# Last expert pair of a two-layer decoder trunk: the residual enters the sums as identity products, and the output copies are shared by two engines

## The reference, cut to what matters

```python
x = x + mla_mixer(...)
h = rmsnorm(x, ffn_norm_o[i])
x = x + moe_swiglu(h, ...)      # the output of the program

# moe_swiglu: top 2 of 8 experts for each token
for e in range(N_EXPERTS):
    y = y + combine[:, e:e + 1] * (silu(ht @ w_gate[e]) * (ht @ w_up[e])) @ w_down[e]
```

## Time and profile before

| | us |
|---|---|
| median of 3 runs (lowest, highest) | 1339.09 (1338.69, 1341.25) |
| profiled execution | 1338.47 |
| its span, first to last instruction | 1336.3 |
| TensorE busy (share of the span) | 1276.0 (95%) |
| VectorE busy | 749.7 (56%) |
| ScalarE busy | 633.7 (47%) |
| mean of HBM traffic | 316 GB/s |

### The profile page before, as it was taken

One profiled execution on the slowest core, in us unless ns is written; L12 is line 12 of the kernel. 1 busy time (PEld: TensorE's weight loads), 2 busy tenths in 40 slices (PEclk: granted clock), 3 DMA queues, 4 the chain that ended last, 5 costly groups with the idle time before them and its releaser, 6 DMA issues.

```text
span 1336.3 us, 15885 instructions
## 1 busy us (share of the span) xinstructions
PE 1276.0 (95%) x6208; PEld 899.4 (67%) x6209; DVE 749.7 (56%) x933; ACT 633.7 (47%) x730; POOL 39.0 (3%) x48
## 2 busy tenths in 40 slices
PE   7987999999987989999999999999999999999997
PEld 6765788888875778475847565766656675838572
DVE  5876465444487458464727464736646543837370
ACT  5575562434358537263626353625444533626350
POOL 1012000000002200000000000000000000000000
PEclk9998999999998979999999999999999999999999
DMA  9632455364353458799999999999999999999996
GB/s 341 222 127 65 155 189 189 116 228 149 103 165 136 189 213 318 305 390 411 421 421 421 421 417 417 421 421 420 421 418 417 420 421 420 421 418 418 420 421 251
DMA packets 88757, 422.92 MB, mean 316 GB/s; under 512 B 8561, under 2 KB 15463, under 8 KB 57959
## 3 DMA queue, kind: packets, MB, share of 16 engines
q1 hardware_dynamic: 87468, 419.10, 79.5%
q0 software_dynamic: 992, 2.69, 0.6%
q10 hardware_dynamic: 218, 0.08, 0.0%
HBM read 420.77 MB, written 1.07 MB: 316 GB/s over the span
## 4 chain that ended last, share of the span: by engine, by line
PE 84%; DVE 7%; DMA 4%; ACT 3%; issue 2%; SPq 0%; DVEq 0%; ACTq 0%
PE PS L2151 12%; PE PS L2127 11%; PE PS L2131 11%; PE PS L2128 11%; PE PS L2143 7%; PE PS L1696 7%; PE PS L1700 7%; PE PS L1697 7%; DMA raw<-in_w_down_o_dram 3%; DVE w_r L954 2%; PE PS L2158 1%; PE PS L2067 1%; PE PS L2076 1%; ACT w_r L487 1%; PE PS L1815 1%
## 5 line engine op out<-in xcount | busy, mean ns | idle before, releaser
L1377 DVE TENSOR_TENSOR w_r<-raw,w_r 128x2048 fp32r<-128x2048 f32 (+1 forms) x150 | 314.8, 2102 | 179.3 <-ACT w_r L784 178.8
L784 ACT ACTIVATE w_r<-raw 128x2048 fp32r<-128x2048 f32 (+1 forms) x150 | 264.9, 1766 | 205.9 <-PE PS L2131 118.6
L2127 PE MATMUL PS<-w_r,a_hi 128*128 128x512 f32 x512 | 201.8, 394 | 0.0
L2128 PE MATMUL PS<-w_r,a_lo 128*128 128x512 f32 x512 | 199.9, 390 | 0.0
L2151 PE MATMUL PS<-raw,xs 128*64 128x512 f32 (+1 forms) x856 | 169.9, 543 | 0.0
L954 DVE TENSOR_TENSOR w_r<-raw,w_r 128x2048 fp32r<-128x2048 f32 (+4 forms) x69 | 139.3, 2044 | 40.2 <-ACT w_r L487 40.0
L1696 PE MATMUL PS<-w_r,a_hi 128*128 128x512 f32 (+4 forms) x384 | 144.4, 380 | 6.0 <-DVE a_lo L983 5.1
L1697 PE MATMUL PS<-w_r,a_lo 128*128 128x512 f32 (+4 forms) x384 | 141.9, 373 | 0.0
L487 ACT ACTIVATE w_r<-raw 128x2048 fp32r<-128x2048 f32 (+4 forms) x69 | 115.2, 1719 | 15.4 <-PE PS L1700 12.6
L2151 PEld LDWEIGHTS PS<-raw,xs 128*64 128x64 f32 x856 | 58.8, 137 | 92.8 <-issue 84.2
L2127 PEld LDWEIGHTS PS<-w_r,a_hi 128*128 128x128 f32 x512 | 96.2, 188 | 28.0 <-issue 8.5
(11 more groups left out here) (318 smaller groups left out, 1445.9 us busy)
## 6 DMA issues: line engine op xcount, KB each, us to landing
raw<-in_w_down_o_dram SPq DMA_DIRECT2D x94, 1024.0 KB, 18.8
raw<-in_w_gate_o_dram SPq DMA_DIRECT2D x53, 1024.0 KB, 14.6
raw<-in_w_up_o_dram SPq DMA_DIRECT2D x51, 1024.0 KB, 15.1
raw<-in_w_gate_o_dram SPq DMA_DIRECT2D x53, 768.0 KB, 12.1
raw<-in_w_up_o_dram SPq DMA_DIRECT2D x53, 768.0 KB, 11.7
slots<-in_w_down_o_dram SPq DMA_DIRECT2D x18, 1024.0 KB, 18.3
raw<-in_w_in_e_dram SPq DMA_DIRECT2D x12, 1024.0 KB, 10.5
raw<-in_w_down_e_dram SPq DMA_DIRECT2D x11, 1024.0 KB, 4.8
```

Source lines behind the costliest of these rows:

```text
L784: nc.scalar.activation(w_r[:, high_slot(g), 0:w], place_of(n)[:, 0:w], ACT.Copy).then_inc(hi_done, 1)
L1377: nc.vector.tensor_tensor(place_r(n)[:, 0:w], place_of(n)[:, 0:w], w_r[:, high_slot(g), 0:w], ALU.subtract).then_inc(lo_done, 1)
L2127: nc.tensor.matmul(PS[:, bank, :], xh(x), hi[:, c0:c0 + NT], start=first, stop=False)
L2128: nc.tensor.matmul(PS[:, bank, :], xl(x), hi[:, c0:c0 + NT], start=False, stop=False)
```

## The change

In the last pair TensorE makes back_large four chunks earlier (behind k = 84), and behind it four more products, ident times the matching piece of X, into the same four banks. The sums that back_small closes therefore hold the new X already. VectorE's four additions go; VectorE copies banks 0 and 2 to X, ScalarE copies banks 1 and 3. A new semaphore out_act counts ScalarE's copies, and the stores, TensorE's last wait and the spare pass wait for both counts. The spare pass, which this input doesn't run, uses the semaphores raw_full in place of seven of its own.

```diff
+        F_SPARE = [16 * len(range(i, C_MOE, RAW)) for i in range(RAW)]
+        LAST_ADDS = 4 * (PAIRS - 1) + 2
@@ SyncE @@
-                    .then_inc(sem(f"spare_full{slot}"), 16)
+                    .then_inc(raw_full[slot], 16)
...
             for s in range(4):
                 t, half = s // 2, s % 2
-                sp.wait_ge(sem("moe_add"), 4 * (PAIRS - 1) + s + 1)
+                sp.wait_ge(sem("out_act" if half else "moe_add"), t + 1 if half else 4 * (PAIRS - 1) + t + 1)
@@ ScalarE, end of pair(p, follow) @@
                 small_result(p)
+                if not follow:
+                    for s in (1, 3):
+                        act.wait_ge(sem("moe_sc"), 4 * p + s + 1)
+                        nc.scalar.activation(X[:, s // 2, NT:D], PS[:, LAST_BACK[s], :], ACT.Copy).then_inc(sem("out_act"), 1)
@@ VectorE, end of pair(p, follow) @@
                 if not follow:
-                    for s in range(4):
-                        add_back(p, s, LAST_BACK[s])
+                    for s in (0, 2):
+                        dve.wait_ge(sem("moe_sc"), 4 * p + s + 1)
+                        nc.vector.tensor_copy(X[:, s // 2, 0:NT], PS[:, LAST_BACK[s], :]).then_inc(sem("moe_add"), 1)
@@ TensorE, pair(p, follow) @@
-                    if not follow and k == PAIR_CHUNKS - 4:
+                    if not follow and k == PAIR_CHUNKS - 8:
                         pe.wait_ge(sem("s_es"), 4 * p + 4)
                         back_large(p, LAST_BACK)
+                        pe.wait_ge(sem("moe_add"), 4 * p)
+                        for s in range(4):
+                            nc.tensor.matmul(PS[:, LAST_BACK[s], :], ident, X[:, s // 2, s % 2 * NT:(s % 2 + 1) * NT],
+                                             start=False, stop=False)
@@ TensorE, behind the last pair @@
-            pe.wait_ge(sem("moe_add"), 4 * PAIRS)
+            pe.wait_ge(sem("moe_add"), LAST_ADDS)
+            pe.wait_ge(sem("out_act"), 2)
```

More of the change, by code:

```diff
@@ L450, in _ @@
             with sp.If(most > 0):
-                sp.wait_ge(sem("moe_add"), 4 * PAIRS)
+                sp.wait_ge(sem("moe_add"), LAST_ADDS)
+                sp.wait_ge(sem("out_act"), 2)
                 with sp.Fori(0, NE) as e:
@@ L461, in _ @@
                         for slot in range(RAW):
-                            sp.sem_inc(sem(f"spare_full{slot}"), 16 * SPARE_CHUNKS // RAW)
+                            sp.sem_inc(raw_full[slot], 16 * SPARE_CHUNKS // RAW)
                 sp.wait_ge(sem("spare_add"), 4 * NE)
@@ L871, in pair @@
                 small_result(p)
+                if not follow:
+                    for s in (1, 3):
+                        act.wait_ge(sem("moe_sc"), 4 * p + s + 1)
+                        nc.scalar.activation(X[:, s // 2, NT:D], PS[:, LAST_BACK[s], :], ACT.Copy).then_inc(sem("out_act"), 1)
             def spare(i):
                 for k in range(SPARE_CHUNKS):
-                    act.wait_ge(sem(f"spare_full{k % RAW}"), 16 * (k // RAW + 1) + i * (16 * SPARE_CHUNKS // RAW))
+                    act.wait_ge(raw_full[k % RAW], F_SPARE[k % RAW] + 16 * (k // RAW + 1) + i * (16 * SPARE_CHUNKS // RAW))
                     act.wait_ge(mm_done, M_SPARE + k - STG + 1 + i * SPARE_CHUNKS)
@@ L915, in _ @@
             with act.If(most > 0):
-                act.wait_ge(sem("moe_add"), 4 * PAIRS)
+                act.wait_ge(sem("moe_add"), LAST_ADDS)
                 with act.Fori(0, NE) as e:
```

## The result

The changed kernel takes 1342.60 us (median of 8 runs, 1341.45 to 1344.59) where the kernel before takes 1339.12 (median of 8, 1337.25 to 1342.84). The ratio is 1.0027, with a 95% interval of 1.0016 to 1.0037: slower by 3.5 us, between 2.1 and 5.0. The profiled execution took 1341.98 us, its span is 1340.2.

A forecast was written before the change was run, and what follows sets the result against it. The prediction took TensorE to set the last stretch and, through its queue, the end; 3.47 us for products less 0.8 from the tail gave +2.67, or 1341.1 to 1341.8 us, forecast 1341.5, range 1339.4 to 1343.6.

The forecast's parts named there:

- The sum: Whole change: 3.47 us for the products less 0.8 from the tail, +2.67 us.
- if the branch grew by as much as the copies saved: Named sign of error at TensorE's last branch, expected near 3.4 us while the copies end 0.92 us earlier.
- TensorE sets the stretch, so all of the products lies on the path: Small down products behind the last large chunk: TensorE doesn't wait for weights, so added products cost their full 3.47 us.
- Rival B: Behind k = 84: products fill a wait for late weights, only the 0.8 to 0.92 gain remains, 1338.3 us; chance 0.04.
- 3.47 us for four products: Identity products on TensorE: two float32 records of 0.43 to 0.45 us each, 3.44 to 3.6 in all, 3.47 taken.
- Rival C: Identity products cheap: 0.23 us each, about 1339, or in pairs, about 1339.8; chance 0.04.
- Moving back_large costs 0: back_large four chunks earlier: same eight products, inputs ready long before, banks free; cost 0.
- The last copy ends 0.92 us earlier: Copies on VectorE and ScalarE side by side: TensorE's wait ends at 1330.2 us and not 1331.1.
- TensorE's queue, not the stores, sets the end: End of span: last piece of X written plus 5.2 us through TensorE's queue, stores with about 1.5 us to spare.
- 0.8 of the 0.92 arrives: TensorE's load and branch at the end start 0.92 us earlier, 0.8 is left as gain; bounds 0 and 0.95.
- the 0.12 us taken off for the instruction packet: TensorE's last branch: 0.12 us deducted for an instruction packet that may stand behind some of the stores.
- Rival A: Tail gives nothing back: instruction packet queues behind stores or copies hinder each other; net +3.5, 1342.3 us; chance 0.13.

The follow-up runs named there:

- e1: The changed kernel without the four identity products, the residual left out of the output; ratio to the kernel before 0.9991.
- e6: The changed kernel with the identity products behind the last small down product instead of behind back_large; ratio to the kernel before 1.0015.
- e8: The kernel before with back_large behind k = 84 in place of k = 88, nothing else; ratio to the kernel before 1.0010.
- e4: The kernel before with need read at k = 88 and TensorE branching right behind back_small, its wait inside the spare pass; ratio to the kernel before 0.9996.
- e5: The changed kernel with need read at k = 84 and TensorE branching right behind back_small, its waits inside the spare pass; ratio to the kernel before 1.0025.
- e3: The changed kernel with four stores of 32 columns each in place of 512; ratio to the kernel before 1.0018.
- e2: The changed kernel with all four copies on VectorE, none on ScalarE; ratio to the kernel before 1.0032.

## Why the prediction was right or wrong

The direction and the range were right: 1342.6 measured, 1341.5 predicted, 1339.4 to 1343.6 the range, "slower" the likeliest of the three. The sum was +2.67; the medians give +3.5, with an interval (2.1 to 5.0) that holds the sum. But one sign of being wrong that the prediction named, "if the branch grew by as much as the copies saved", came true: 0.94 us against 0.93. That the total fits all the same is in part luck, as the last two points show.

- *TensorE sets the stretch, so all of the products lies on the path.* Right: 3.43 us added with e1 as the counterpart, and 0.66 less where TensorE would have been idle (e6). Rival B falls. (The page's DMA row reaches 9 tenths only behind slice 16 of 40, and its last slice has 6; nothing rests on it, since the end was read by its own rows.)
- *3.47 us for four products.* Right within 0.04. The records last 592 ns and the eight take 3.43, the lower end of the range worked out from the 512-column rows. (In that working the 256-column record gives 0.22, not 0.215; nothing hangs on it.) Rival C falls. By the Trainium skill, "VectorE: DVE Perf Modes", section "The TRN2 errata", an estimated 0.86 us would have come out; the trace does not agree for float32.
- *Moving back_large costs 0.* Right (e8).
- *The last copy ends 0.92 us earlier.* Right: 1.55 behind the first's start, 2.48 before. The Trainium skill, "PSUM — Partial Sum Buffer", section "Specifications (TRN2)", says that ScalarE and VectorE can access PSUM in parallel at full bandwidth as long as they don't collide on a bank. The trace agrees closely: 692 and 598 ns side by side in different banks, against 692 and 579 in the earlier trace rows.
- *TensorE's queue, not the stores, sets the end.* Right for both kernels: e4 and e5 take TensorE out of it, and the end moves to SyncE.
- *0.8 of the 0.92 arrives, the branch staying near 3.4 us.* This is the step that failed, and in it the 0.12 us taken off for the instruction packet. The branch took 4.376 us, the end came 5.96 us behind the last copy where 5.2 was expected, and SyncE waited 1.5 us for TensorE, not under 1.2. I had the price from a packet among weights, which took 1.08 us in place of 0.99, and so looked at its duration; what grew was the time until it started, from 1.0 to 1.9 us behind the branch. Most of that goes away without the stores (e3, where the branch is 0.65 us shorter). Within the span 0.16 arrived in this pair of profiles. Over all six that end with TensorE's branch and full stores, the tails of one engine (7.67, 7.88, 7.82) lie 0.34 above those of two (7.51, 7.41, 7.43). Rival A, the tail gives nothing back, came half true.
- *Span and time differ by a constant.* Not said, but assumed (the span was forecast to move by the same 2.67). All runs with both engines copying have 1.76 to 1.94 us outside the span, all runs with one engine 2.11 to 2.26, and e2 shows that the copies make the difference: about 0.35 us. Counted to the whole time the tails are 9.85, 10.05, 9.99 against 9.32, 9.23, 9.25: a gain of 0.70, near the 0.8 that was summed; but only 0.34 of it came by the way that was predicted, so that this nearness is luck. So 3.43 - 0.70 = 2.73 would be the change by pieces; the medians' 3.5 is above it within its interval. Why less lies outside the span stays open.

## What to carry to other kernels

Work moved to the engine that bounds a stretch costs its full length there, however idle the engine that it is taken from will be; here VectorE's additions were 2.5 us at the very end, and replacing them bought 0.7 for 3.4. Before a tail is shortened, follow the span to its last instruction through every engine's queue, the branches over unused code too: a chain of waits that stops at the last compute instruction hides what comes behind it. And where a late step fetches anything, ask what traffic it moves into when it starts sooner.

## What the runs showed of the hardware that was not expected

- A float32 product of 128 x 128 by 512 columns takes 0.86 us of TensorE (3.43 / 4), 3.7 times a product of the high/low kind (0.23); with 64 columns of weights, two run side by side at 0.43 each.
- A branch over an unused pass costs TensorE 3.35 to 4.4 us at the end of this program. Until its instruction packet starts it is 0.9 to 1.2 us where the branch comes ahead of the stores, at their end or with small ones, and 1.4 to 1.9 where it comes in their midst; from there on it is 2.4 to 2.9.
- A 16 KB instruction packet that starts 2.3 to 3.7 us behind the first issue of 1 MB of stores goes with a last landing 0.8 to 1.1 us later, in five profiles of five; that it is the cause isn't shown.
- Where ScalarE makes two of the last four copies, 1.8 us of the execution lie outside the span; where VectorE makes all, 2.2. Why stays open.
- Identical work up to the last 14 small chunks reaches them at times 5.7 us apart (1297.9 to 1303.6) in twelve profiles; what follows repeats to 0.01 us up to the first copy or addition.
